# Modulation in blocks of two feature tiles, and the sum of squares shared by two engines

## What is computed

```
def _rms_norm(x, g):
    xf = x.astype(jnp.float32)
    y = xf * lax.rsqrt(jnp.mean(xf * xf, axis=-1, keepdims=True) + EPS)
    return (y * g.astype(jnp.float32)).astype(x.dtype)

def _ada(cond, w, b):
    m = jax.nn.silu(cond) @ w + b
    return jnp.split(m, 3, axis=-1)

def _prologue(x, ctx, c, c_ctx, g, w_mod, b_mod):
    sh, sc, gt = _ada(c, w_mod, b_mod)
    shc, scc, gtc = _ada(c_ctx, w_mod, b_mod)
    hx = _rms_norm(x, g) * (1 + sc[:, None]) + sh[:, None]
    hc = _rms_norm(ctx, g) * (1 + scc) + shc
    h = jnp.concatenate([hc, hx], axis=1)
    return h, gt[:, None], gtc
```

## Time and profile before

| | us |
|---|---|
| median of 3 runs | 1211.07 (1210.99 to 1212.01) |
| profiled execution | 1209.13 |
| its span | 1207.3 |
| TensorE busy | 1159.2 (96%) |
| VectorE busy | 825.5 (68%) |
| ScalarE busy | 498.4 (41%) |
| GpSimd busy | 422.1 (35%) |

### The profile page before, as it was taken

How to read it: one execution, slowest core, us unless ns; L and a number is a source line. 1 busy time by engine, 2 the same in 40 slices (tenths; PEclk the granted TensorE clock), 3 DMA queues, 4 the chain that set the end, 5 groups by cost and what they waited for, 6 DMA issues and landing times.

```text
span 1207.3 us, 16923 instructions
## 1 busy us (share of the span) xinstructions
PE 1159.2 (96%) x6610; PEld 956.2 (79%) x6610; DVE 825.5 (68%) x1264; ACT 498.4 (41%) x924; POOL 422.1 (35%) x330
## 2 busy tenths in 40 slices
PE   3899999999999999999999999999999999999996
PEld 2678879887888987878888888876877777777885
DVE  5699839989925356136839968249888888884237
ACT  3445455220014542134523442246666666664012
POOL 4800000000000002532211112248888888887232
PEclk9899999999999999999999999999999999999998
DMA  9934776425521846203121122330000000000403
GB/s 340 363 114 133 181 221 243 140 91 207 175 88 53 294 176 231 70 36 124 51 70 36 36 79 79 88 122 9 10 18 10 18 18 10 19 9 27 156 26 132
DMA packets 81023, 129.83 MB, mean 108 GB/s; under 512 B 12944, under 2 KB 43024, under 8 KB 80144
## 3 DMA queue, kind: packets, MB, share of 16 engines
q1 hardware_dynamic: 71120, 113.96, 28.2%
q10 hardware_dynamic: 9824, 14.80, 3.5%
HBM read 97.81 MB, written 30.93 MB: 107 GB/s over the span
## 4 chain that ended last, share of the span: by engine, by line
PE 82%; DVE 13%; DMA 2%; ACT 2%; issue 1%; POOL 1%; ACTq 0%; DVEq 0%
PE ps L1860 9%; PE ps L1862 9%; PE ps L1861 9%; PE ps L1871 5%; PE ps L1872 5%; PE ps L1873 5%; DVE region_d L1113 3%; PE ps L2144 3%; PE ps L2174 3%; PE ps L2173 3%; PE ps L2172 3%; PE ps L2222 2%; PE ps L2224 2%; PE ps L2223 2%; PE ps L2193 2%; PE ps L2191 2%
## 5 line engine op out<-in xcount | busy, mean ns | idle before, releaser
L675 POOL TENSOR_TENSOR region_b<-region_b,region_d 128x512 f32<-128x512 f32 x20 | 26.3, 1329 | 472.0 <-DVE region_d L1513 472.0
L1860 PE MATMUL ps<-w_hi,a_hi 128*128 128x512 f32 x448 | 177.7, 397 | 5.6 <-DVE b_lo L1201 4.3
L1861 PE MATMUL ps<-w_lo,a_hi 128*128 128x512 f32 x448 | 175.4, 392 | 0.0
L1862 PE MATMUL ps<-w_hi,c_lo 128*128 128x512 f32 x368 | 143.3, 389 | 0.0
L1871 PE MATMUL ps<-a_hi,w_hi 128*128 128x512 f32 (+1 forms) x384 | 138.0, 359 | 0.0
L1872 PE MATMUL ps<-b_lo,w_hi 128*128 128x512 f32 (+1 forms) x384 | 136.0, 354 | 0.0
L1873 PE MATMUL ps<-a_hi,w_lo 128*128 128x512 f32 (+1 forms) x384 | 136.0, 354 | 0.0
L668 POOL TENSOR_TENSOR w_lo<-weight_ring,w_hi 128x2048 fp32r<-128x2048 f32 x14 | 65.1, 4650 | 185.5 <-ACT w_hi L724 185.5
L1607 DVE TENSOR_REDUCE small<-ps 128x1 f32<-128x1280 f32 x64 | 95.0, 1484 | 40.2 <-PE ps L2144 40.2
L697 POOL TENSOR_TENSOR region_c<-region_c 128x512 f32<-128x512 f32 x80 | 110.0, 1375 | 28.1 <-ACT region_c L1084 25.4
L1860 PEld LDWEIGHTS ps<-w_hi,a_hi 128*128 128x128 f32 x448 | 84.8, 189 | 25.3 <-issue 6.3
(11 more groups left out here) (250 smaller groups left out, 2671.5 us busy)
## 6 DMA issues: line engine op xcount, KB each, us to landing
weight_ring<-in_w_mod SPq DMA_DIRECT2D x10, 2048.0 KB, 9.1
weight_ring<-in_we_in SPq DMA_DIRECT2D x10, 1024.0 KB, 5.6
weight_ring<-in_wo_in SPq DMA_DIRECT2D x10, 1024.0 KB, 5.2
weight_ring<-cop_t_scratch SPq DMA_DIRECT2D x4, 1536.0 KB, 8.4
region_c<-in_w_mod SPq DMA_DIRECT2D x2, 2048.0 KB, 20.9
bop_scratch<-region_d ACTq DMA_DIRECT2D x16, 256.0 KB, 2.9
cop_t_scratch<-region_d SPq DMA_DIRECT2D x8, 512.0 KB, 7.8
weight_ring<-bop_scratch SPq DMA_DIRECT2D x2, 2048.0 KB, 9.8
```

Source lines behind the costliest of these rows:

```text
L1860: te.matmul(o, th, wh[:, k % 4], start=k == 0, stop=False)
L1861: te.matmul(o, th, wl[:, k % 4], start=False, stop=False)
L1862: last = te.matmul(o, tl, wh[:, k % 4], start=False, stop=k == KT - 1)
```

## The change

- The columns of w_mod's first layer are laid out anew, so that block e holds 256 shifts and 256 scales, those of feature tiles 2e and 2e+1. Blocks are taken in the order 0, 1, 2, 3, and `half_evac` becomes `pair_evac`, run four times, each behind one block.
- TensorE takes the column sums and the broadcast first, then block 0. Block 1 goes between the first v matmuls of tiles 0 and 1, block 2 between those of tiles 2 and 3, block 3 behind all 72.
- GpSimd adds the squares of half 0 ahead of its parameter chain, VectorE those of half 1, and VectorE waits for GpSimd before it adds the halves.
- The second exp moves on VectorE behind the pair of tiles 0 and 1.
- SP loads ("v", 0) ahead of block 0, and ScalarE rounds it ahead of the square root.

```
-        M = [("mod0", b) for b in (0, 2, 1, 3, 4, 5)] + [("mod1", b) for b in range(6)]
+        M = [("mod0", b) for b in range(6)] + [("mod1", b) for b in range(6)]
...
+            ring_load("v", 0)
             ring_load(*M[0])
-            ring_load("v", 0)
             ring_load(*M[1])
...
+            pool.wait_ge(s_sq, 1)
+            for m in (2, 1):
+                tt(XQ[:, 0:m, 0:T01], XQ[:, 0:m, 0:T01], XQ[:, m:2 * m, 0:T01], ALU.add)
+            param_ops.append(n[0])
             pool.wait_ge(s_exp, 1)
...
-            mod_row(0)
+            act.wait_ge(s_consts, 2)
+            weights_round(("v", 0))
             act.wait_ge(s_ss_mm, 1)
-            act.wait_ge(s_consts, 2)
             a.activation(rstd[:, 0:6], sums, ACT.Sqrt, bias=epsc, scale=1.0 / D).then_inc(s_rt, 1)
-            weights_round(("v", 0))
             act.wait_ge(s_bc_mm, 1)
             copy(rstd_rows[:, 0:T01], rows01).then_inc(s_bc_ok, 1)
-            mod_row(1)
-            gained_round(0, range(4), 0)
-            gained_round(1, range(4), 4)
+            for e in range(2):
+                mod_row(e)
+                gained_round(0, (2 * e, 2 * e + 1), 4 * e)
+                gained_round(1, (2 * e, 2 * e + 1), 4 * e + 2)
             mod_row(2)
...
-            for e in range(2):
-                dve.wait_ge(s_sq, e + 1)
-                for m in (2, 1):
-                    z = XQ[:, 4 * e:4 * e + m, 0:T01]
-                    step(v.tensor_tensor(z, z, XQ[:, 4 * e + m:4 * e + 2 * m, 0:T01], ALU.add))
+            dve.wait_ge(s_sq, 2)
+            for m in (2, 1):
+                z = XQ[:, 4:4 + m, 0:T01]
+                step(v.tensor_tensor(z, z, XQ[:, 4 + m:4 + 2 * m, 0:T01], ALU.add))
+            dve.wait_ge(s_pchain, param_ops[0])
             v.tensor_tensor(XQ[:, 0, 0:T01], XQ[:, 0, 0:T01], XQ[:, 4, 0:T01], ALU.add).then_inc(s_pre, 1)
-            exp_(mg, xe)
...
-            half_evac(0)
-            gained(0, range(4))
-            gained_rest(0, range(4), 0)
-            for k in range(4):
-                gained(1, (k,))
-                gained_rest(1, (k,), 4 + k)
+            for e in range(2):
+                pair_evac(e)
+                pair = (2 * e, 2 * e + 1)
+                gained(0, pair)
+                gained_rest(0, pair, 4 * e)
+                for k in pair:
+                    gained(1, (k,))
+                    gained_rest(1, (k,), 2 * e + 2 + k)
+                if e == 0:
+                    exp_(mg, xe)
             weights_rest(("v", 1))
-            half_evac(1)
-            gained(0, range(4, KT))
-            gained_rest(0, range(4, KT), 8)
+            for e in (2, 3):
+                pair_evac(e)
+                gained(0, (2 * e, 2 * e + 1))
+                gained_rest(0, (2 * e, 2 * e + 1), 4 + 2 * e)
...
-            mods(0)
-            mod_cols(0)
             pe.wait_ge(s_pre, 1)
             for t in range(6):
                 last = te.matmul(sums[:, t:t + 1], XQ[:, 0, P * t:P * t + P], onec, start=True, stop=True)
             last.then_inc(s_ss_mm, 1)
             rstd_across(0)
-            mods(1)
-            mod_cols(1)
+            mods(0)
+            mod_cols(0)
...
-            for k in range(4):
-                pe.wait_ge(s_h_lod, k + 1)
-                for t in range(2):
-                    v_part(t, (k,))
-            mods(2)
-            for k in range(4):
-                pe.wait_ge(s_h_lod, k + 5)
-                for t in range(2, 6):
-                    v_part(t, (k,))
-                if k == 0:
-                    mod_cols(2)
-                    mods(3)
-                if k == 1:
-                    mod_cols(3)
+            for e in range(2):
+                for k in range(2):
+                    pe.wait_ge(s_h_lod, 4 * e + k + 1)
+                    for t in range(2):
+                        v_part(t, (2 * e + k,))
+                mods(e + 1)
+                for k in range(2):
+                    pe.wait_ge(s_h_lod, 4 * e + k + 3)
+                    for t in range(2, 6):
+                        v_part(t, (2 * e + k,))
+                    if k == 0:
+                        mod_cols(e + 1)
+            mods(3)
+            mod_cols(3)
...
+    laid["w_mod"] = inputs["w_mod"].copy()
+    laid["w_mod"][0][:, 0:2 * D] = inputs["w_mod"][0][:, np.arange(2 * D).reshape(2, 4, QC).transpose(1, 0, 2).reshape(2 * D)]
```

More of the change, by code:

```diff
@@ L1171, in weights_rest, with pair_evac @@
                 v.tensor_tensor(wl, slot_raw(u), wh.bitcast(F32), ALU.subtract).then_inc(s_w_lo, 1)
-            def half_evac(e):
-                dve.wait_ge(s_mod_tr, 2 * e + 2)
-                v.tensor_tensor(modc[0][:, 0:16].rearrange("p (a e b) c -> p e a b c", a=2, e=2)[:, e],
-                                ps[:, 7, 256 * e:256 * e + 256].rearrange("p (a b c) -> p a b c", a=2, c=32)[:, :, :, 0:2],
-                                bmod[0][:, 0:16].rearrange("p (a e b) -> p e a b", a=2, e=2)[:, e].unsqueeze(3).broadcast_to([P, 2, 4, 2]),
+            def pair_evac(e):
+                dve.wait_ge(s_mod_tr, e + 1)
+                v.tensor_tensor(modc[0][:, 0:16].rearrange("p (a e b) c -> p e a b c", a=2, e=4)[:, e],
+                                ps[:, 7, P * e:P * e + P].rearrange("p (a b c) -> p a b c", a=2, c=32)[:, :, :, 0:2],
+                                bmod[0][:, 0:16].rearrange("p (a e b) -> p e a b", a=2, e=4)[:, e].unsqueeze(3).broadcast_to([P, 2, 2, 2]),
                                 ALU.add).then_inc(s_mod_ev, 1)
                 dve.wait_ge(s_mod_ev, e + 1)
-                ks = slice(4 * e, 4 * e + 4)
-                ts(hA[0][:, ks], modc[0][:, 8 + 4 * e:12 + 4 * e], 1.0, ALU.add)
-                v.tensor_tensor(hA[0][:, ks], hA[0][:, ks], ng[0][:, ks].unsqueeze(2).broadcast_to([P, 4, 2]), ALU.mult).then_inc(s_mod_ok, 1)
+                ks = slice(2 * e, 2 * e + 2)
+                ts(hA[0][:, ks], modc[0][:, 8 + 2 * e:10 + 2 * e], 1.0, ALU.add)
+                v.tensor_tensor(hA[0][:, ks], hA[0][:, ks], ng[0][:, ks].unsqueeze(2).broadcast_to([P, 2, 2]), ALU.mult).then_inc(s_mod_ok, 1)
                 dve.wait_ge(s_mod_ok, e + 1)
@@ L1745, in mod_cols @@
                     pe.wait_ge(s_bc_ok, 2)
-                if m in (2, 4, 6, 10):
-                    pe.wait_ge(s_mod_ev, {2: 1, 4: 2, 6: 3, 10: 4}[m])
+                if m in (1, 2, 3, 4, 6, 10):
+                    pe.wait_ge(s_mod_ev, {1: 1, 2: 2, 3: 3, 4: 4, 6: 5, 10: 6}[m])
                 i = m % 6 % 4
@@ L1969, in _ @@
             pe.wait_ge(s_mod_row, 12)
[L1970 removed]
+            pe.wait_ge(s_mod_ev, 7)
             gt_rows(0, 0, 6, s_gt_tr)
```

9 lines of the change are left out of this document (4 added, 5 removed).

## The result

The changed kernel takes 1222.01 us (median of 6 runs, 1218.78 to 1225.36), the kernel before beside it 1211.44 (1208.67 to 1212.01). The ratio is 1.0091 [1.0068, 1.0114]. The forecast was 1221.9 with a range of 1216.0 to 1225.5 and 0.92 for slower. The profiled execution took 1225.36 with a span of 1223.5. So it lies 3.35 above its median, while the profile of before lies 2.3 under its own: the two traces differ by 16.2 us, the medians by 10.6.

A forecast was written before the change was run, and what follows sets the result against it. It took VectorE's normalized tiles as the bound from 14.8 to 116 us. First product +0.1, block 3's place and tail +9.9 and clock +0.8 sum to +10.8: 1219.9 profiled, median 1221.9, range 1216.0 to 1225.5.

The forecast's parts named there:

- Q: Twelfth low part, which lets TensorE start the second half of v (59.11 before); claimed to move by +10.0 us.
- From S to the first product: Same steps in the same order as before, so first v product on TensorE at 34.35 against 34.26.
- S: Start of the 12 column-sum records on TensorE, 22.93 before; forecast 23.55, +0.6 us.
- G: Start of the first normalized tile on VectorE, 32.04 before; forecast 32.65.
- The tail behind block 3: ScalarE's row, four squares and roundings, then VectorE's low parts, behind block 3's end: from 59.9 to 69.0.
- Passing on: Behind Q, same work in the same order with triggers from these engines, so 10.0 us passes on.
- third sign: Prediction wrong if the time from the second half's first v product to the end isn't about 1148.2 us.
- Rival 1: VectorE is not stopped by GpSimd's adds, all up to Q 3.8 us earlier: +7.0; chance 0.18.
- rival 2: TensorE's clock is up at 2.4 GHz in the first half: +7.1, with Rival 1 +3.3; chance 0.07.
- rival 4: Faster: TensorE starts so early that block 3 ends by 49.9; 1 us gained (1210.0) with squares away; chance 0.03.
- Rival 3: Delay given back later, at a wait for a load that did not move: 0 to +3; chance 0.05.
- rival 5: More: block 1 at low clock (+1.15), exp stretched (+1.5), clock loss uncovered (+2.0): +13 to +15; chance 0.05.

The follow-up runs named there:

- e1: Changed kernel with TensorE's block 3 moved ahead of the last twelve matmuls of the first half: 1220.61 us, ratio 1.0065 to before.
- e2: Changed kernel with ScalarE's four squares and their root ahead of the row of block 3: 1217.64 us, ratio 1.0050 to before.
- e3: Changed kernel with all adds of squares back on VectorE: 1218.89 us, ratio 1.0052 to before.
- e7: Changed kernel with GpSimd's two adds replaced by six memsets that write the same region and read nothing: 1222.07 us, ratio 1.0082 to before.
- e9: Changed kernel once more, unedited, for a second profile: median of two runs 1225.15 us, ratio 1.0112 to before.
- e8: Kernel before once more, unedited, for a second profile: 1211.16 us, ratio 0.9996.
- e12: Kernel before with one added wait on SP, so four 0.5 MB copies are issued behind TensorE's lag products: 1211.73 us, ratio 0.9999.
- e4: Changed kernel with the edits of e1, e2 and e3 together: 1214.88 us, ratio 1.0022 to before.
- e10: Changed kernel with one added wait on SP, so four 0.5 MB copies are issued behind TensorE's lag products: 1223.83 us, ratio 1.0093 to before.
- e6: e5 with ScalarE's squares behind the rounding of tiles 4 to 7 and what needs them one token tile later: 1210.17 us, ratio 0.9998 to before.
- e5: Changed kernel's two-tile blocks with the old head: block 0 first, adds and second exp as before, blocks 2 and 3 early: 1211.81 us, ratio 1.0003 to before.
- e11: e6 with one added wait on SP, so four 0.5 MB copies are issued behind TensorE's lag products: 1210.94 us, ratio 0.9994 to before.

## Why the prediction was right, and where its terms were off

**The bound, right.** Q was named as the place to compare, and block 3 with ScalarE's squares behind it as what would end last. Both are in the trace, and e1, e2 and e3 each take one cause away and move Q by 3.05, 4.55 and 3.10 (of the last, 2.06 are the adds).

**The stop of VectorE by GpSimd, right.** GpSimd's adds took 5.35 (forecast 3.51 + 1.85), the exponential chain ended at 19.72 (forecast 19.75), the column sums began at 23.65 (23.55). e7 shows that reading makes the difference for the two-input instructions. In the first profile the stopped ones are other than assumed, the second of a pair from 11.85 and a TENSOR_SCALAR; in e9 they are the assumed ones (the six in 5.97). The sum is the same, since each stop ends with one of GpSimd's adds.

**From S to the first product, off by 1.2.** "The same steps in the same order as S to G before": the steps are, their length isn't. From S to G it was 10.23 instead of 9.11, from G to the first product 1.73 (forecast 1.7). The column sums take 1.47 in the first profile of before, 2.56 in its two others (e8, e12), and 2.69 in all eight profiles in which TensorE had done nothing ahead of them (changed, e1 to e4, e7, e9, e10). So only 0.13 of it can be laid to the block that was taken from in front of them: e8 has 10.21 from S to G in the kernel before itself. The prediction took as fixed a duration read from one execution, and a short one. Up to Q this is the largest term that was mis-sized.

**TensorE in the first half, right.** 35.61 to 61.34 is 25.73; forecast was 23.65 + 1.94 = 25.59. Block 1 took 2.25 instead of 1.93, in the slow stretch. In e9 the same stretch took 24.43 (35.94 to 60.37), so the term holds to 1.3 us.

**The tail behind block 3, a little long.** 9.1 us were forecast from its end (59.9) to 69.0 for the last low part, 8.6 came (61.34 to 69.93). From the row to the first rounding it is 4.66 instead of 5.02, and the rest was as listed. With +1.26 at the first product, +0.14 in the half and -0.47 in the tail, Q is at +10.97 instead of +10.0. In e9, with other parts (+1.59, -1.16, -0.47), it is at +10.0.

**Loads, exp and the parameter chain, right at nothing.** ScalarE rounds the v weights at 16.26 (forecast 15.9) without a visible effect, SP's load of ("v", 1) is issued at 32.48, exp stands at 40.20 to 43.9, and GpSimd's parameter chain ends at 61.48 (2.4 later; forecast 2.7) with its reader past 76.

**The clock, +1.1 instead of +0.8.** From Q to the lags of half 2 the delay grows from 10.97 to 12.09; in e9 it grows only from 10.00 to 10.41, so the forecast lies between two executions.

**Passing on, right but not whole.** "10.0 passes on" holds up to 147 us. Then the issue wait adds 2.35 and the clock behind it some 1.3 (at the transposes +16.02 = 12.09 + 2.35 + 1.58; the rest is not split further). No step of the prediction had it, though its row (1.16 us of issue) stood in the chain of before. In the changed kernel it is 3.51 and 3.64 in two profiles. By its third sign the prediction called itself wrong if the time from Q to the end isn't about 1148.2: it is 1153.4, and 1154.8 in e9. Of these 5.2 us more, some 1.1 are the clock (0.8 forecast) and 3.9 the issue wait with what follows it, so this step held only up to 147 us.

**The total, partly by luck.** The sum from the steps was +10.8, the traces have +16.2, the medians +10.6. The profiles of before (1209.13) and of the changed kernel (1225.36) lie at opposite ends of their runs, as the issue wait lies at opposite lengths in them. That the sum and the medians agree to 0.2 us is chance: six runs of the changed kernel spread over 6.6, and with e9's two runs the medians are 12.5 apart. A good part of the spread between executions is at this place: from the start of the lags of half 2 to the transposes the fourteen profiles have 34.3 to 40.0 us, from there to the end 1025.6 to 1027.7. e12, which is as fast as before, shows in its profile 2.25 us of wait and the clock at a half for some 6 us behind it, with a span of 1212.2 where before has 1207.3 with 1.16 us and no fall. That the runs of the changed kernel with the shorter times had the shorter wait was not seen, since only one execution of each is profiled. The time outside the span varies as well, from 1.8 us in most runs to 3.5 in single ones.

**The rivals.** Rival 1 (no stop) fell by the rows at 11.85; rival 2 (the clock is up) by the windows; rival 4 (faster) had block 3 end by 49.9 as its condition, and it ended at 61.34. Its idea isn't wrong in itself: e6 reaches that state (block 3 ends at 41.9 there, with the squares out of the way) and still its median shows no gain clear of noise; in its profile the 2.3 us that VectorE gains by 76 us are gone behind the wait at 152. The gain of 1 us (1210.0) that the prediction gave for this case is neither shown nor excluded. Rival 3 is nearest to what came on top: +3.9 behind 147 us, though by a wait of kind "issue" and not for a load. Of rival 5, the exp took 3.7 us, inside its cover. Block 1 took 2.25, +0.3 instead of +1.15.

## What to carry to other kernels

When a step moves behind the last cover on its engine, count not only the step but all that its reader's queue holds between it and the next thing that is waited for: TensorE stood 8 us behind a block of 1.93 us here, 4.5 of them for four squares behind its row. Take a short chain's duration from more than one execution: the same column sums took 1.47 and 2.56 us in one kernel, and 1.1 us of the forecast hung on it. And before a small gain is believed or given up, follow it past the next wait of kind "issue" and the clock behind it, in more than one profile; the 2.3 us of e6 were there at 147 us and not at 182, but the kernel before itself moves by 4 us there.

## What the runs showed of the hardware

- GpSimd instructions that only write do not hold up VectorE's two-input instructions (six in 1.32 us beside memsets), but they do hold up TENSOR_SCALAR and CAST on as few as 32 elements: 0.95 to 1.48 us instead of 0.18. Beside adds, which read, the same six two-input instructions took 5.97.
- TensorE waits 0.68 to 3.64 us for nothing visible at the same place of its program (behind 2497 of its records) in all fourteen profiles, and goes on 2.25 to 2.94 us behind the start of a packet of the instruction queue, also when the copies beside it are moved. That queue moves one packet of 16 KB for some 254 matmuls and weight loads (52 for 13220). Behind the eleven waits of 1.73 us and more the granted clock fell; behind 0.68, 1.16 and 1.41 (e5, before, e8) it stayed at 1.00.
- Twelve column-sum matmul records of one column took 1.40 or 1.47 us (before, e6, e11) or 2.56 (e5, e8, e12) where a block stood ahead of them on TensorE, and 2.69 in eight profiles with an idle TensorE ahead of them.
